# Moving the PSUM eviction of convolution chunks to ScalarE, their Silu one chunk later, and two norm steps later

## The reference

```
h = rmsnorm(x, norm1_g) * (1 + sc1) + sh1
proj = jnp.einsum('btd,de->bte', h, w_in)
q, k, v, o, ig, fg, z, xbc, dt = jnp.split(proj, bounds, axis=-1)
qk, conv_a1 = causal_conv_silu(jnp.concatenate([q, k], axis=-1), conv_a0, conv_a_w, conv_a_b)
xbc, conv_b1 = causal_conv_silu(xbc, conv_b0, conv_b_w, conv_b_b)
...
y_b = y_b.reshape(bsz, T, D_B) * jax.nn.silu(z.astype(f32))
y_b = rmsnorm(y_b, ssm_norm_g).astype(x.dtype)
```

## Time and profile before

| | us |
|---|---|
| median of 3 runs | 2476.29 (2473.99 to 2479.18) |
| profiled execution | 2475.14 |
| its span, first to last instruction | 2473.3 |
| PE busy | 2306.3 (93%) |
| DVE busy | 1542.1 (62%) |
| POOL busy | 1131.0 (46%) |
| ACT busy | 876.1 (35%) |

### The profile page before, as it was taken

How to read it: one execution, slowest core, us unless ns; L and a number is a source line. 1 busy time by engine, 2 the same in 40 slices (tenths; PEclk the granted TensorE clock), 3 DMA queues, 4 the chain that set the end, 5 groups by cost and what they waited for, 6 DMA issues and landing times.

```text
span 2473.3 us, 33195 instructions
## 1 busy us (share of the span) xinstructions
PE 2306.3 (93%) x12935; PEld 1956.2 (79%) x12935; DVE 1542.1 (62%) x2594; ACT 876.1 (35%) x1145; POOL 1131.0 (46%) x555
## 2 busy tenths in 40 slices
PE   5899998967997999999999989999999999999998
PEld 4898888855746987787778878888788888888886
DVE  4676677563714147877889787775465555555552
ACT  3424444561122133333335544455332322322221
POOL 1342235235423336566566675555554444444441
PEclk8999999987998999999999999999999999999999
DMA  7122122555654355555556897677564544555540
GB/s 267 60 79 70 56 71 69 153 167 173 204 170 117 89 131 144 136 145 137 137 134 175 229 270 193 175 194 193 212 269 188 201 179 181 200 204 193 197 153 34
DMA packets 307350, 392.67 MB, mean 159 GB/s; under 512 B 14490, under 2 KB 257582, under 8 KB 302859
## 3 DMA queue, kind: packets, MB, share of 16 engines
q1 hardware_dynamic: 212107, 302.86, 40.6%
q10 hardware_dynamic: 91664, 75.54, 9.4%
q0 software_dynamic: 3456, 12.58, 1.6%
HBM read 305.70 MB, written 81.26 MB: 156 GB/s over the span
## 4 chain that ended last, share of the span: by engine, by line
PE 54%; DVE 4%; POOL 3%; DMA 2%; ACT 1%; issue 1%; ACTq 0%; DVEq 0%
PE bank L2570 28%; PE bank L2027 22%; PE bank L2521 3%; DVE work L2247 2%; POOL utL_hid L2017 2%; DMA work<-sample_rows_dram 2%; DVE work L2250 1%; PE bank L2526 1%; POOL work L2205 1%; DVE ut_hid L2006 1%; PE bank L2508 0%; DVE work L2320 0%; ACT utH_hid L2013 0%; POOL work L2175 0%; POOL work L1948 0%
## 5 line engine op out<-in xcount | busy, mean ns | idle before, releaser
L2017 POOL TENSOR_TENSOR utL_hid<-ut_hid,utH_hid 128x1024 fp32r<-128x1024 f32 x128 | 346.1, 2704 | 327.3 <-ACT utH_hid L2013 326.7
L2027 PE MATMUL bank<-pH,utH_hid 128*128 128x512 f32 x1024 | 406.3, 397 | 13.5 <-POOL utL_hid L2017 13.5
L2027 PE MATMUL bank<-pH,utL_hid 128*128 128x512 f32 x1024 | 399.3, 390 | 0.0
L2027 PE MATMUL bank<-pL,utH_hid 128*128 128x512 f32 x1024 | 399.2, 390 | 0.0
L2570 PE MATMUL bank<-area,work 128*128 128x512 f32 x1536 | 350.8, 389 | 0.0
L2570 PEld LDWEIGHTS bank<-area,work 128*128 128x128 f32 x1536 | 288.5, 188 | 59.7
L864 PE MATMUL ps_in<-hH_in,wH_in 128*128 128x260 f32 x816 | 239.4, 293 | 16.9 <-POOL wL_in L824 15.5
L2006 DVE STREAM_TRANSPOSE ut_hid<-u_hid 128x1024 f32<-128x1024 f32 x128 | 158.8, 1241 | 150.9 <-POOL utL_hid L2017 132.0
L2183 POOL TENSOR_TENSOR pL<-work,pH 128x1024 fp32r<-128x1024 f32 x64 | 155.1, 2424 | 193.7 <-ACT pH L2426 193.7
L824 POOL TENSOR_TENSOR wL_in<-wb_in,wH_in 128x1024 fp32r<-128x1024 f32 x52 | 129.1, 2484 | 249.1 <-ACT wH_in L777 249.1
L2027 PEld LDWEIGHTS bank<-pH,utH_hid 128*128 128x128 f32 x1024 | 192.6, 188 | 56.2 <-POOL utL_hid L2017 18.7
(11 more groups left out here) (526 smaller groups left out, 4442.1 us busy)
## 6 DMA issues: line engine op xcount, KB each, us to landing
u_hid<-in_peer_u_dram SPq DMA_DIRECT2D x256, 256.0 KB, 5.0
work<-in_peer_v_dram SPq DMA_DIRECT2D x64, 1024.0 KB, 5.0
hidden_dram<-ge_hid ACTq DMA_DIRECT2D x64, 512.0 KB, 3.0
gates_dram<-area ACTq DMA_DIRECT2D x16, 2048.0 KB, 10.5
wb_in<-in_w_in_dram SPq DMA_DIRECT2D x26, 1024.0 KB, 5.3
wstage<-in_w_ada_dram SPq DMA_DIRECT2D x32, 512.0 KB, 5.2
wstage<-in_w_out_dram SPq DMA_DIRECT2D x16, 1024.0 KB, 5.1
area<-hidden_dram SPq DMA_DIRECT2D x16, 1024.0 KB, 6.8
```

What stands on the lines that cost most here:

```text
L2017: self.nc.gpsimd.tensor_tensor(self.utL[:, u % 2], self.ut[:, u % 2], self.utH[:, u % 2].bitcast(F32), ALU.subtract).then_inc(self.low, 1)
L2027: mm = self.nc.tensor.matmul(self.pa[u % 2][:, :], w[:, u % 2, k, :], x[:, k, :], start=(n == 0), stop=(n == 3 * KD - 1))
```

## The change

```diff
--- before.py
+++ after.py
@@ -623,7 +623,7 @@
         if k < 2 and s:
             f = 2 * (s - 1) + k
             dve.wait_ge(m["t_in"], f + 1)
-            dve.wait_ge(self.z_in, f + 1)
+            dve.wait_ge(self.z_in, 12 + f + 1)
             z = S.proj[:, NZ + f, 0:T]
             V.tensor_tensor(z, self.px[:, :], z, ALU.mult).then_inc(m["t_out"], 1)
         if s == self.SUBS:
@@ -717,7 +717,7 @@
     chunks += out_gates[0:6]
     chunks += [(c * P, NQ + c, "conv", (c, V_CAW + c, 16, V_CAB + c)) for c in range(16)]
     chunks += out_gates[6:8]
-    on_act = [not isinstance(kind, str) for _, _, kind, _ in chunks]
+    on_act = [kind != "copy" for _, _, kind, _ in chunks]
     before = lambda n, act: sum(1 for i in range(n) if on_act[i] == act)
     convs = lambda n: sum(1 for i in range(n) if chunks[i][2] == "conv")
     hooks = {2 * (first_z + 4 * s) + k: (s, k) for s in range(Ssd.SUBS) for k in range(8)}
@@ -743,7 +743,7 @@
         z_sum = S.rb[:, 0:T]
         z_sq = lambda f: z_sum if f == 0 else y[:, f % 2, :] if f < 6 else S.proj[:, NX + f - 6, 0:T]
         z_done = {first_z + 4 * (f // 2) + 4: (f, f + 1) for f in range(0, KD, 2)}
-        Z_ROOT, Z_NORM, Z_GAIN = first_q + 4, first_q + 5, first_q + 6
+        Z_ROOT, Z_NORM, Z_GAIN = first_q + 4, first_q + 7, first_q + 8
         block = ctx.enter_context(nc.Block())
         split = lambda slot: S.proj[:, slot, :].rearrange("p (a n) -> p a n", a=2)
 
@@ -783,17 +783,17 @@
             for n, (_, slot, kind, _) in enumerate(chunks):
                 if n + 2 < len(chunks):
                     move_high(n + 2)
-                if kind == "conv":
-                    act.wait_ge(convd, convs(n) + 1)
-                    x = S.proj[:, slot, 0:T]
-                    silu = nc.scalar.activation(x, y[:, convs(n) % 2, :], ACT.Silu)
-                    if first_k <= n < first_k + 8:
+                if on_act[n]:
+                    act.wait_ge(product, n + 1)
+                    nc.scalar.activation(split(slot), ps[n % 2][:, :, 0:HN], ACT.Copy if kind == "conv" else kind).then_inc(by_act, 1)
+                if n and chunks[n - 1][2] == "conv":
+                    act.wait_ge(convd, convs(n - 1) + 1)
+                    x = S.proj[:, chunks[n - 1][1], 0:T]
+                    silu = nc.scalar.activation(x, y[:, convs(n - 1) % 2, :], ACT.Silu)
+                    if first_k <= n - 1 < first_k + 8:
                         own(silu)
                         silu = nc.scalar.activation(x, x, ACT.Copy, scale=KSCALE)
                     silu.then_inc(used, 1)
-                elif on_act[n]:
-                    act.wait_ge(product, n + 1)
-                    nc.scalar.activation(split(slot), ps[n % 2][:, :, 0:HN], kind).then_inc(by_act, 1)
                 if n == 0:
                     B0.keep_gates(act, own)
                 for part, at in enumerate((0, 1, 5, 6)):
@@ -888,7 +888,7 @@
                     dve.wait_ge(used, c - 1)
                 if c in (12, 13):
                     dve.wait_ge(z_added, c - 8)
-                dve.wait_ge(by_dve, before(n + 1, False))
+                dve.wait_ge(by_act, before(n + 1, True))
                 tap = lambda j: S.vec[:, taps + j * stride:taps + j * stride + 1]
                 V.tensor_copy(S.raw[:, raw, :], x[:, T - 3:N])
                 own(V.tensor_scalar(yc, x[:, 0:T], tap(3), S.vec[:, bias:bias + 1], ALU.mult, ALU.add))
```

## The result

| us | before | after |
|---|---|---|
| median of 5 runs each | 2478.26 | 2462.28 |
| profiled execution | 2475.14 | 2465.41 |
| its span | 2473.3 | 2463.6 |
| first matmul of the main loop (L864) | 68.1 | 67.7 |
| first matmul of the mLSTM phase (L974) | 454.9 | 436.5 |

A forecast was written before the change was run, and what follows sets the result against it. TensorE, the busiest engine, was taken as the bound, with 15.5 us of waits for POOL's weights; gains of 7.8 + 9.65 + 3.4 = 20.9 us take 2475.14 to 2454.3, as a median 2455, range 2449 to 2463.

The forecast's parts named there:

- The filter is late next: In the conv chunks, VectorE's filter would be late next, holding Silu and ScalarE's next rounding and eviction; 4.7 us spare.
- nearly vanish: Sign: ScalarE's wait for VectorE's filter, which sat in front of the rounding of weights, should nearly vanish.
- full blocking: Rival, chance 0.10: VectorE and POOL exclude each other wholly, 6.7 us a late chunk, TensorE waits 3.3 us: 2458.
- The first stall: Rival, chance 0.09: VectorE's gate rows come so late that chunk 8 still starts at low clock; 7.8 us lost: 2463.
- the slower case: Rival, chance 0.04: TensorE waits about 1 us at each of eight chunks and each wait drops the clock: 2485.
- hold each other up, but not fully: Late chunks: VectorE and POOL delay each other only partly, so a chunk costs VectorE 6.0 us, 0.3 over TensorE's pace.
- the spare 4.7 us of the round trip: Late chunks: eviction to the chunk three further on takes 12.4 us of 17.1 available, leaving 4.7 us as cover.
- first conv chunks: 7.8 us: Waits before chunks 7 and 8 shrink from 0.80 and 5.13 to 0.9 us, and 2.8 of clock returns: 7.8 gained.
- its clock term of 2.8: Chunk 8, after its stall, took 8.5 us instead of 5.7 at low clock; these 2.8 us would come back.
- the term of 3.4 for the late chunks: Chunks 41 to 49: TensorE sets the pace at 5.7 us a chunk, so 3.4 us come back.
- Later phases only start earlier: Behind the barrier ending the input projection, later phases start some 21 us earlier and take as long as before.
- its own terms: The forecast's own range: gains from 18 to 23 us, and some 2.5 us either way for single runs' spread.

The follow-up runs named there:

- after_third: The changed kernel run once more with nothing altered, for a third profile: median 2462.68 us, ratio 0.9939 against the kernel before.
- all eight profiles named above: Four profiles of the changed kernel and four of variants with the same front; clock 0.50 to 0.74 over the first 2.6 us behind chunk 9's gate block.

## Why the prediction was wrong in its sum, and where it was right

**The mechanism was right in the main.** TensorE's 15.5 us of waits fell to 1.2 (forecast about 1), the wait before chunk 8 is 0.79 (0.9), the gate row ended at 104.35 (between 102.6 and 105.0; POOL's subtraction did fall onto it, and one 8x8 step of VectorE took 2.35 us in place of 0.15), chunks 8 and 40 run at full clock, and the eviction costs 0.59 (0.60). The filter is late next, as said: it holds ScalarE up to 5.1 us in the late chunks, and TensorE loses 0.39 to it. My words that this wait would "nearly vanish" were wrong; only its cost vanished. The first stall and the slower case did not come. Of full blocking the price did not come, but the blocking did: that the engines "hold each other up, but not fully" was read from rows that merge three filter steps, and step by step VectorE and POOL do shut each other out (last section). The rival's 6.7 us a chunk was too long: ScalarE evicted chunk 44 at 395.18 and chunk 46 at 407.39, 6.1 a chunk, and the spare 4.7 us of the round trip took the lag up, so TensorE lost 0.39 and not 3.3.

**The sum was too high.** By stretches of the two first profiles, from one eviction or end of a chunk to the next:

| stretch | before | after | gain | forecast |
|---|---|---|---|---|
| chunk 0's eviction to chunk 17's | 112.60 | 106.34 | 6.3 | 7.8 |
| to chunk 33's | 155.15 | 155.14 | 0.0 | 0 |
| to the end of chunk 40 | 50.60 | 40.64 | 10.0 | 9.65 |
| to the first matmul of the next phase | 68.83 | 67.03 | 1.8 | 3.4 |

The first step that failed is "first conv chunks: 7.8 us", by its clock term of 2.8. Up to the block behind chunk 9 the gain was (130.79 - 67.72) - (122.53 - 67.30) = 7.8, exactly the forecast. But the clock that chunk 8 got back was lost again behind the block, 1.6 us in after and 3.0 in after_third: I counted the clock of one stall by itself and not what the engine's later light stretches would do without it. The second is the term of 3.4 for the late chunks, "TensorE sets the pace": it took the whole excess over 5.7 us a chunk as gain. From the end of chunk 40 to that of chunk 49 it took 421.86 - 369.42 = 52.4 us, 5.83 a chunk, against 54.9 before, so 2.5 came, and 0.39 of what is missing is the wait before chunk 48. Behind chunk 49 another 0.7 was lost, 0.5 of it in the longer wait for the next phase (3.1 against 2.6).

**The rest.** "Later phases only start earlier" held within their spread of 4 to 9 us, and in the means failed by some 1.8, without a known cause. And the forecast started from 2476.29, the median of three runs, while 65 runs have a mean of 2478.0. Together: 2455.4, and 1.7 for the base, 20.9 - 17.8 = 3.1 for the loop, 0.4 for its start and 1.8 behind it give 2462.4, the mean of the 16 runs. That this lies within 2463 is luck: the range reaches so far up only for the stall before chunk 8, which did not stay, and its own terms, gains of 18 to 23 and 2.5 either way, give 2450.8 to 2460.8. Its lower end of 2449 follows from no term.

## What to carry to other kernels

Look in an in-order queue for work that waits for something far away and stands ahead of work that the busiest engine needs; moving it one step back can be worth more than any saving, while moving work onto that queue without doing so can close a ring (here 32 us slower). Price a stall's clock loss together with the stretches of little matmuls that follow it, since a clock given back at one place can be lost at the next. And before reading a difference behind the change, profile both kernels several times: here one pair of profiles suggested a loss of 8.7 us that was mostly spread. Read instructions one by one before judging how two engines hold each other up: a merged row of three showed a slowdown where single steps were shut out.

## What the runs showed of the hardware

Behind a block of 3.3 us of little matmuls without a gap the granted clock went to 0.50 for 3 to 6 us, in all eight profiles named above, and where the block was put, the fall went too. Two transposes of 8 or 16 rows between three large matmuls cost 0.42 us, three times what they cost in a block.

And the rule of the shared port pair, which the prediction weighed (the Trainium skill, SBUF — State Buffer, "Who interferes with whom"), held here for VectorE instructions that read two inputs from SBUF as well as for a copy within SBUF. In the late chunks of after each of them that began beside a POOL operation ended at that operation's end or a little later. The copy of 128x11 that starts a filter took 1.92 us beside POOL's subtraction, and ended where that ended, against 0.16 with POOL idle. Of the filter's steps, 0.75 us each with POOL idle (three take 2.32), the one that began beside the subtraction at 387.74 took 2.79 and ended 0.55 behind it; the next began beside the product and took 1.67, ending 0.55 behind that. The product, which began while the step before still ran, took 1.74 in place of 1.28. So the 5.28 us of three steps are not a slower pace but two waits, which count as part of the instruction. At the first conv chunks the same made the 8x8 step of the gate rows 2.35 us long, against 0.15 in before, where POOL was idle. Evictions out of PSUM were not held: 0.68 to 0.70 us in before, also where they lay wholly beside a POOL operation. VectorE's timeline, and POOL's:

```profile
100.12 2.35 DVE L475 TENSOR_TENSOR projarea<-projarea,m0T 8x8 f32<-8x8 f32 x1
...
387.89 2.79 DVE L897 SCALAR_TENSOR_TENSOR y_in<-projarea,vec,y_in 128x510 f32<-128x510 f32 x1
390.71 1.67 DVE L897 SCALAR_TENSOR_TENSOR y_in<-projarea,vec,y_in 128x509 f32<-128x509 f32 x1
392.30 0.16 DVE L893 COPY raw<-projarea 128x11 f32<-128x11 f32 x1
...
395.87 1.92 DVE L893 COPY raw<-projarea 128x11 f32<-128x11 f32 x1 [0.60 <-ACT projarea L788]
```

```profile
387.74 2.39 POOL L824 TENSOR_TENSOR wL_in<-wb_in,wH_in 128x1024 fp32r<-128x1024 f32 x1 [1.15 <-ACT wH_in L777]
390.09 1.74 POOL L839 TENSOR_TENSOR projarea<-projarea,rb 128x512 f32<-128x512 f32 x1
...
395.35 2.41 POOL L824 TENSOR_TENSOR wL_in<-wb_in,wH_in 128x1024 fp32r<-128x1024 f32 x1 [3.52 <-ACT wH_in L777]
```
